# The decoder step's cached-value sums read two steps ahead, and the convolution norm's squares added on VectorE

## What is computed

```
q, k, v, f, a, gate = split(x @ w_in)                    # cd_in: 20 tiles of 128 channels
# branch C: attention with forget gates, 8 heads of 64
prompt: causal softmax(q k' / 8 + c_t - c_s) v           # 4 head pairs x 4 query blocks = 16 units
sample: the same over 2048 cached rows in 16 pages each, read through page_table
# branch D: convolution module
u = a * sigmoid(gate)
y = depthwise_conv31(u) + conv_b
y = silu(layernorm(y) over 512 channels)                 # mean and variance over 4 channel rows of 128
out = concat(attention, y) @ w_out                       # cd_out
```

## Time and profile before

| what | value |
|---|---|
| median of 3 runs | 1365.25 us (1364.73 to 1366.31) |
| the profiled execution | 1366.27 us |
| its span, first to last instruction | 1364.4 us |
| TensorE busy | 1322.3 us, 97% of the span |
| VectorE, ScalarE, GpSimd busy | 785.9, 452.1, 538.7 us |
| mean granted TensorE clock | 0.990 |

### The profile page before, as it was taken

One profiled execution on the slowest core, in us unless ns is written; L12 is line 12 of the kernel. 1 busy time (PEld: TensorE's weight loads), 2 busy tenths in 40 slices (PEclk: granted clock), 3 DMA queues, 4 the chain that ended last, 5 costly groups with the idle time before them and its releaser, 6 DMA issues.

```text
span 1364.4 us, 28531 instructions
## 1 busy us (share of the span) xinstructions
PE 1322.3 (97%) x11630; PEld 1255.3 (92%) x11630; DVE 785.9 (58%) x1013; ACT 452.1 (33%) x601; POOL 538.7 (39%) x240
## 2 busy tenths in 40 slices
PE   7999999999999999999999989999999999999996
PEld 7999999999999999999989973479999999999996
DVE  3256784787655553232788997647687555550045
ACT  3331233433332222121434235544433333231122
POOL 2342432456555555333300011013365555654351
PEclk9999999999999999999999989999999999999998
DMA  6222241233333333222689979962223333232211
GB/s 251 62 84 73 65 108 51 80 81 96 95 95 94 89 101 102 92 92 62 207 318 298 340 268 338 394 255 87 85 77 92 92 92 90 84 123 86 91 37 62
DMA packets 84572, 180.47 MB, mean 132 GB/s; under 512 B 25993, under 2 KB 26122, under 8 KB 83986
## 3 DMA queue, kind: packets, MB, share of 16 engines
q1 hardware_dynamic: 83810, 175.50, 39.2%
q0 software_dynamic: 688, 3.92, 0.9%
HBM read 173.33 MB, written 6.05 MB: 131 GB/s over the span
## 4 chain that ended last, share of the span: by engine, by line
PE 82%; DVE 9%; SPq 4%; ACT 2%; issue 2%; DMA 1%; ACTq 0%; DVEq 0%
PE ps L1089 75%; SPq L382 3%; DVE pj L2342 2%; PE ps L1480 1%; PE ps L1238 1%; DVE wl L2384 1%; DVE pj L2223 0%; DMA pages<-in_cache_v 0%; DVE pj L2216 0%; DMA raw<-in_w_ab_in 0%; SPq L372 0%; PE ps L1342 0%; PE ps L1597 0%; ACT x L554 0%; DVE hid_t L1901 0%
## 5 line engine op out<-in xcount | busy, mean ns | idle before, releaser
L922 POOL TENSOR_TENSOR wl<-raw,wh 128x1024 fp32r<-128x1024 f32 (+1 forms) x163 | 450.9, 2766 | 513.1 <-ACT wh L437 513.1
L1089 PE MATMUL ps<-xh,wh 128*128 128x260 f32 x2112 | 435.3, 287 | 16.2 <-DVE xl L1873 9.2
L1089 PE MATMUL ps<-xl,wh 128*128 128x260 f32 x2112 | 429.2, 284 | 0.0
L1089 PE MATMUL ps<-xh,wl 128*128 128x260 f32 x2112 | 428.9, 284 | 0.0
L437 ACT ACTIVATE wh<-raw 128x1024 fp32r<-128x1024 f32 (+1 forms) x179 | 199.9, 1117 | 542.8 <-PE ps L1089 542.4
L1089 PEld LDWEIGHTS ps<-xh,wh 128*128 128x128 f32 x2112 | 330.6, 190 | 23.2 <-issue 18.1
L1089 PEld LDWEIGHTS ps<-xl,wh 128*128 128x128 f32 x2112 | 330.2, 190 | 0.0
L1089 PEld LDWEIGHTS ps<-xh,wl 128*128 128x128 f32 x2112 | 329.2, 190 | 0.0
L1089 PE MATMUL ps<-hh,wh 128*128 128x260 f32 x704 | 142.1, 283 | 0.0
L1089 PE MATMUL ps<-hh,wl 128*128 128x260 f32 x704 | 141.5, 282 | 0.0
L1089 PE MATMUL ps<-hl,wh 128*128 128x260 f32 x704 | 141.3, 282 | 0.0
(11 more groups left out here) (362 smaller groups left out, 1467.0 us busy)
## 6 DMA issues: line engine op xcount, KB each, us to landing
raw<-in_w_f_in SPq DMA_DIRECT2D x88, 512.0 KB, 3.6
pages<-in_cache_kt SPq DMA_DIRECT2D x128, 256.0 KB, 4.5
pages<-in_cache_v SPq DMA_DIRECT2D x128, 256.0 KB, 4.7
raw<-in_w_f_out SPq DMA_DIRECT2D x32, 704.0 KB, 4.0
raw<-in_w_ab_in SPq DMA_DIRECT2D x23, 512.0 KB, 3.6
raw<-in_w_cd_in SPq DMA_DIRECT2D x20, 512.0 KB, 5.5
raw<-in_w_ab_out SPq DMA_DIRECT2D x8, 512.0 KB, 3.6
raw<-in_w_cd_out SPq DMA_DIRECT2D x8, 512.0 KB, 6.5
```

The costliest lines, as they stand in the source:

```text
L922: nc.gpsimd.tensor_tensor(wl[:, j % SPLIT, 0:b * P], raw[:, j, 0:b * P], wh[:, j % SPLIT, 0:b * P].bitcast(F32), ALU.subtract).then_inc(w_ ...
L1089: mm = nc.tensor.matmul(out[h], w[:, slot, block_at * P:block_at * P + P], rows[k][:, HT * h:end if h else HT], start=start and a, stop=st ...
```

## The change

It has four parts. TensorE takes page slots 0 to 3 ahead of step 0, and step n then takes 2n + 4 and 2n + 5, so that steps 14 and 15 have none. `scores(0)` moves into slot (4,2) of cd_in, and with it go `cached_exps(0)`, `exps(0)`, `stage_p(0)` and `stage_p(1)`, and `unit_max(0)`; eight taps go from slots (4,2) and (4,3) to the steps. SP issues cd_out's weight slots 2 and 3 behind all value pages. VectorE adds the squares of the four channel rows into one, and TensorE sums that one row.

```diff
-TAPS_BESIDE = {... (4, 2): 7, (4, 3): 7}
-STEP_TAPS = (4, 4, 4, 4, 4, 4, 4, 4, 4, 4, 4, 4, 4, 0, 0, 0)
+TAPS_BESIDE = {... (4, 2): 3, (4, 3): 3}
+STEP_TAPS = (5, 5, 5, 4, 5, 5, 4, 5, 4, 5, 4, 5, 4, 0, 0, 0)
...
# SP
-                    weight_slot(name, k, j)
+                    if name == "cd_in" or j < SPLIT:
+                        weight_slot(name, k, j)
...
             with sp.Fori(1, NB) as b:
                 values(b)
+            for j in range(SPLIT, RAW):
+                weight_slot("cd_out", 0, j)
             weights("cd_out", 1)
...
# ScalarE: at_slot runs beside each slot of cd_in
+                if (i, j) == (4, 3):
+                    exps(0)
...
+                if (i, j) == (4, 2):
+                    cached_exps(0)
...
-            cached_exps(0)
-            value_tokens(0)
-            value_tokens(1)
-            exps(0)
-            value_tokens(2)
-            value_tokens(3)
             probabilities(0)
+            for c in range(4):
+                value_tokens(c)
...
# TensorE
                 elif (i, j) == (4, 2):
                     maxima_cast(0, 4)
+                    scores(0)
...
             def conv_variance(h):
-                pe.wait_ge(cv_sq, h + 1)
-                pe.wait_ge(cv_centered, h + 1)
-                for k in range(4):
-                    mm = nc.tensor.matmul(ps[:, 6 - h, 0:HT], ones, squares_d[:, k, HT * h:HT * h + HT], start=k == 0, stop=k == 3)
-                mm.then_inc(cv_var, 1)
+                pe.wait_ge(cv_sq, 4)
+                nc.tensor.matmul(ps[:, 6 - h, 0:HT], ones, squares_d[:, 0, HT * h:HT * h + HT], start=True, stop=True)\
+                    .then_inc(cv_var, 1)
-            scores(0)
+            value_slot(0)
+            value_slot(1)
             turn_scores(1)
-            for c in range(4):
+            for c in range(3):
                 values_turned(c)
+            value_slot(2)
+            value_slot(3)
+            values_turned(3)
...
-                value_slot(2 * n)
-                value_slot(2 * n + 1)
+                if 2 * n + 4 < 4 * NB:
+                    value_slot(2 * n + 4)
+                    value_slot(2 * n + 5)
...
# VectorE
+                    if (i, j) == (4, 2):
+                        dve.wait_ge(p_all, 1)
+                        for b in range(2):
+                            stage_p(b)
+                        unit_max(0)
...
+            def squares_summed(h):
+                dve.wait_ge(cv_sq, 2 * h + 1)
+                four = squares_d[:, :, cols(h)]
+                link(V.tensor_tensor(four[:, 0:2], four[:, 0:2], four[:, 2:4], ALU.add))
+                V.tensor_tensor(four[:, 0], four[:, 0], four[:, 1], ALU.add).then_inc(cv_sq, 1)
...
-                if n >= 2 and n % 2 == 0 and n // 2 + 1 < NB:
-                    stage_p(n // 2 + 1)
+                if n % 2 == 1 and (n + 3) // 2 < NB:
+                    stage_p((n + 3) // 2)
...
+            squares_summed(0)
             mask_values(1)
+            squares_summed(1)
             keep_past(1)
```

More of the change, by code:

```diff
@@ L48 @@
 STEPS = 16
-TAPS_BESIDE = {(1, 2): 5, (1, 3): 3, (2, 0): 7, (2, 1): 5, (2, 2): 7, (2, 3): 5, (3, 0): 2, (3, 1): 4, (3, 2): 1, (3, 3): 6, (4, 0): 6, (4, 1): 7, (4, 2): 7, (4, 3): 7}
-STEP_TAPS = (4, 4, 4, 4, 4, 4, 4, 4, 4, 4, 4, 4, 4, 0, 0, 0)
+TAPS_BESIDE = {(1, 2): 5, (1, 3): 3, (2, 0): 7, (2, 1): 5, (2, 2): 7, (2, 3): 5, (3, 0): 2, (3, 1): 4, (3, 2): 1, (3, 3): 6, (4, 0): 6, (4, 1): 7, (4, 2): 3, (4, 3): 3}
+STEP_TAPS = (5, 5, 5, 4, 5, 5, 4, 5, 4, 5, 4, 5, 4, 0, 0, 0)
 CONV_AT = 13
@@ L792, in cached_exps, with exps, probabilities @@
                 nc.scalar.activation(s_all[:, 4 * part:4 * part + 4], s_all[:, 4 * part:4 * part + 4], ACT.Exp).then_inc(p_all, 1)
+            def exps(n):
+                w, b = P * (UNIT_TILES[n % 4] + 1), n % 2
+                act.wait_ge(neg_max, n + 1)
+                if n >= 2:
+                    act.wait_ge(p_turned, n - 1)
+                for h2 in range(2):
+                    last = nc.scalar.activation(prob[:, b, h2, 0:w], ps[:, h2, 0:w], ACT.Exp, bias=tiny[:, 2 * b + h2:2 * b + h2 + 1],
+                                                accum_out=tiny[:, 4 + 2 * b + h2:5 + 2 * b + h2])
+                last.then_inc(exp_done, 1)
+            def probabilities(n):
+                w, b = P * (UNIT_TILES[n % 4] + 1), n % 2
+                act.wait_ge(r_ready, n + 1)
+                for h2 in range(2):
+                    last = nc.scalar.activation(prob[:, b, h2, 0:w], prob[:, b, h2, 0:w], ACT.Copy,
+                                                scale=tiny[:, 8 + 2 * b + h2:9 + 2 * b + h2])
+                last.then_inc(p_ready, 1)
             def at_slot(i, j):
+                if (i, j) == (4, 3):
+                    exps(0)
                 if i == 0:
@@ L828, in value_tokens @@
                 nc.scalar.activation(vtok2[:, c, :], ps[:, (2, 3, 4, 2)[c], :], ACT.Copy).then_inc(v_tok, 1)
[L830 to L846, removed]
             def turned_copy(n):
@@ L1459, in turn_scores, with scores @@
                 mm.then_inc(kt_done, 1)
+            def scores(n):
+                pair, tt = n // 4, UNIT_TILES[n % 4]
+                w = P * (tt + 1)
+                if n == 0:
+                    pe.wait_ge(acc_free[0], PH["cd_in"][2] // 2 + 10 + 1)
+                    pe.wait_ge(rows_ready, 1)
+                    pe.wait_ge(cd_done, 12)
+                else:
+                    pe.wait_ge(exp_done, n)
+                for h2 in range(2):
+                    r0 = 64 * h2
+                    nc.tensor.matmul(ps[:, h2, 0:w], pj2[r0:r0 + 64, CD_Q + pair, P * tt:P * tt + P],
+                                     pj2[r0:r0 + 64, CD_K + pair, 0:w], start=True, stop=False)
+                for h2 in range(2):
+                    r0 = 64 * h2 + 32 * (pair % 2)
+                    nc.tensor.matmul(ps[:, h2, 0:w], left_rows[r0:r0 + 32, P * tt:P * tt + P],
+                                     right_rows[pair // 2][r0:r0 + 32, 0:w], start=False, stop=False)
+                for h2 in range(2):
+                    mm = nc.tensor.matmul(ps[:, h2, P * tt:w], ident_b[:], causal_b[:], start=False, stop=True)
+                mm.then_inc(s_ready, 1)
             def key_slots(i, j):
@@ L1542, in values_turned @@
                 mm.then_inc(v_turned, 1)
[L1544 to L1563, removed]
             def turned(n):
@@ L2385, in weight_rest, with unit_max, inverse_sum @@
                                 ALU.subtract).then_inc(w_rest, 1)
+            def unit_max(n):
+                dve.wait_ge(s_ready, n + 1)
+                V.tensor_reduce(tiny[:, n % 2 * 2:n % 2 * 2 + 2], ps[:, 0:2, 0:P * (UNIT_TILES[n % 4] + 1)], AX, ALU.max, negate=True).then_inc(neg_max, 1)
+            def inverse_sum(n):
+                b = n % 2 * 2
+                dve.wait_ge(exp_done, n + 1)
+                V.reciprocal(tiny[:, 8 + b:10 + b], tiny[:, 4 + b:6 + b]).then_inc(r_ready, 1)
             for i in range(1, 5):
@@ L2476, in conv_variance @@
                 V.tensor_scalar(rstd[:, cols(h)], ps[:, 6 - h, 0:HT], 1.0 / 512, None, ALU.mult).then_inc(cv_taken, 1)
[L2478 to L2481, removed]
+            inverse_sum(0)
             add_decay(1)
             maxima(1)
-            inverse_sum(0)
             for n in range(STEPS):
```

## The result

The changed kernel takes 1368.95 us, the median of 22 runs (1365.2 to 1371.38), against 1365.23 us for the kernel before on the same chips. The ratio is 1.0023, with a 95% interval of 1.0015 to 1.0030: 3.1 us slower, between 2.0 and 4.1 (the two medians alone lie 3.7 apart).

The account below looks back on a forecast made before the run. It took the landing of the last of 112 value pages, plus dependent work, as the bound: matmuls ending at 894.1 plus 15.6 start cd_out at 909.7, 2.8 us later, giving 1368.0 us; range 1362.6 to 1370.9.

Parts of the forecast that it names:

- The stream starts earlier: SP's queue at the end of cd_in: first page of values(1) goes out at 813.0 in place of 819.73, 6.7 us earlier.
- no stretch at 0.50 was to be near 812 to 822: Sign in the changed trace: TensorE would show no half-clock stretch there, around the start of the steps.
- How long the stream lasts: Value pages, first issue to last landing: 80.0 us in place of 80.8, last landing at 893.0.
- the lower bound of 78.7: Shortest stream of value pages: 29.4 MB at 397 GB/s, 74.0 us, plus 4.7 for a landing.
- the stream runs at its best: Rival at the DMA engines: pages keep 397 GB/s, stream 78.7 us, kernel 1366.1 us, not slower; chance 0.18.
- the prediction's sign of being wrong (before 891): In the changed trace, a last page slot ending before 891, where 894 was expected, would make the forecast wrong.
- But it is needed earlier too: Last page slot belongs to step 13, not 15; the work behind it until cd_out takes 15.6 us.
- the eight terms of the sum: Work from the last page slot to cd_out: 0.4, 2.9, 1.8, 0.8, 3.5, 1.0, 0.8 and 4.4 us.
- The squares additions: VectorE ahead of the mask: two additions for the first half take 1.0 us, bounds 0.6 and 1.4.
- The clock at the end: Rival: thin work ahead of cd_out makes it begin at half clock, 2.0 us more, 1370.0 us; chance 0.18.
- Costed at nothing: Eight taps moved to the steps, two weight slots behind the pages, early cached_exps(0) and exps(0): all fit in free time.
- 1363.2: Rival: SP's queue alone sets the pace, stream 75.4 us, 1.8 us less, faster or no change; chance 0.16.

Follow-up runs that it names:

- One step ahead: The changed kernel with page slots read one step ahead in place of two, so step 14 takes the last two; 0.9993 to the kernel before.
- the run kept busy: The changed kernel plus eight matmuls of 128 x 256 that nobody reads, in TensorE's pauses ahead of cd_out; 1.0008 to the kernel before.
- the run with four rows and one step ahead: The changed kernel reading one step ahead in place of two, with TensorE again summing four rows of squares; 0.9962 to the kernel before.
- the profile with four rows and two steps ahead: The changed kernel with TensorE again summing the four rows of squares, everything else of the change kept; 1.0008 to the kernel before.

## Why the prediction was near, step by step

- **The stream starts earlier: right.** Forecast 813.0; by the rows it is 814.27 less the 2.03 us by which this execution came late, 812.2. The wait in step 0 for page slots 2 and 3 is there (the trace has 2.05 and 1.49 us). The early `scores(0)` delays the last slot of cd_in by 1.5 us, as costed. One sign failed: no stretch at 0.50 was to be near 812 to 822, and behind those two waits there is one, from 817.0 to 820.4, in place of some 10 us before. The stream does not suffer from it, for the DMA engines stay full (share 1.04).

```profile
818.00:820.00 2.00, 2.00 (x14) 0.75 (x6) 0.00 (x0) 0.00 (x0) 1.57 (x1) 0.50 1.04 373
```

- **How long the stream lasts: mis-sized, and this is the step that failed.** I took 80.0 us, "near the measured end, since the same engines carry the same pages"; it was 77.8, below the lower bound of 78.7. The four other profiles with two steps read ahead have 77.0 to 78.0. The rival "the stream runs at its best" is what happened, and more than it: the bound assumed 397 GB/s, and 29.4 MB at the 404 of the window, with the 4.6 us median to landing of the profile after, are 77.3. SP's waits inside the stream go with it, 1.5 us before, where I took off one, and none after. Over the profiles the stream lasts about a microsecond longer for each microsecond of such waits: 77.0 to 78.0 us in six with at most 0.4 us, about 79 in two with 1.0 and 1.2 (one of them the squares edit alone, 78.8, whose pages go as in the kernel before), 79.7 with 2.2, and 81.7 in two with 3.4 and 3.8. The profile of before, 80.8 us with 1.5, lies 1.5 to 2 us above that; why is not shown. By the same 2.03 us the last page slot ends at 891.1, just short of the prediction's sign of being wrong (before 891).
- **But it is needed earlier too: right.** Forecast 15.6 us, measured 15.35, and right term by term: the chain's rows give 0.4, 3.0, 1.6, 0.9, 3.4, 1.0, 0.7 and 4.4 for the eight terms of the sum. One step ahead cut it to 10.3.
- **The squares additions: right.** 0.69 and 0.43 us, 1.12 in all, against 1.0 taken from the earlier trace rows. The Trainium skill, "VectorE: DVE Perf Modes", section "The TRN2 errata", has a formula for a single-precision addition; the estimate by it is 0.70 and 0.43, and the trace agrees. That they lie on the path is shown by three more pairs of them. The edit's price at full clock was forecast as 0.7 and is 1.05 by the rests of the two traces.
- **The clock at the end: right as a mechanism, but only a rival.** It had a chance of 0.18, against it that "the pauses are each shorter than the one that did it". It falls after pauses of 0.90, 0.82 and 1.28 us; the size, taken as 2.0, is 1.8 in the trace and 2.0 by the run kept busy. No pause was as long as the one I compared with, but three short ones came one behind the other.
- **Costed at nothing: nothing speaks against it.** The weight slots show no worth, and VectorE has room for the taps (15.59 of 20 us busy); the taps were not tried apart.
- **A slip in the rivals.** 1365.25 + 1.1 is 1366.35, not 1366.1, and 1365.25 - 1.8 is 1363.45, not 1363.2. The forecast does not hang on either.

So the sum should have been: the chain's 2.8 us less 2.2 for the shorter stream, 0.8 for its earlier start and 0.2 for the shorter rest, that is -0.4, as the two traces have it (110.17 for 110.55); and 1.8 for the clock. That is 1.4 us against the one profile of before. The runs say 3.1 (2.0 to 4.1). The profile of before lies 1.0 above the median of its runs, that of after on its own; if that microsecond lies in this stage, perhaps in the long stream, the sum is 2.4. No run shows where it lies, so how the rest divides is not settled. That 2.8 met 3.1 is luck in this sense: a stream and a start that were 3 us better than forecast were made up for by a clock that the forecast left to a rival, and by the part that is not settled.

## What to carry to other kernels

Reading ahead moves a transfer's end forward, and also what waits for it: count the work behind the last landing in both orders before counting the gain, and read ahead only as far as keeps the queue from waiting for places. Before taking work from TensorE just ahead of a long product, look for pauses there, and afterwards at the granted clock: here the product's first eleven rows at half clock cost 1.8 us, and the additions that replaced the work about one more. Matmuls that nobody reads are a cheap test of that.

## What was not expected of the hardware

The granted clock fell to 0.50 though no single pause ahead of the fall was longer than 1.28 us, and it stayed there from about 905.8 to 912.6 us, four microseconds into a TensorE that was full again. In the run with four rows and one step ahead it fell with still smaller pauses (0.69 and 0.34 us in the last five microseconds). But pauses alone do not tell when: in the profile with four rows and two steps ahead it stayed at 1.00 behind pauses of 0.90, 0.83 and 0.20 us. What decides between the two is not shown here. The Trainium skill, "TensorE: Matmul & The Clock Gate", section "Why this matters for your kernels", warns of a long idle gap between bursts of matmuls; the 4.46 us before agree with that, and these traces go further, with gaps that are short one by one.
